# One hybrid decoder step on one core: order of the prompt and decode work inside the merged attention loop

## The reference, cut to what matters

```python
# prompt, causal, query blocks of 128
s = einsum('bqhcd,bkhcd->bhcqk', qi, k) * scale      # c: the two sub-heads
a = softmax(where(kpos <= qpos, s, -inf), axis=-1)
w = a[:, :, 0] - lam * a[:, :, 1]
o = einsum('bhqk,bkhv->bqhv', w, v)
# decode, per sequence: past pages and the new tokens under one softmax
s_past = einsum('bqhcd,bkhcd->bhcqk', q, k_past) * scale
s_new = where(tril, einsum('bqhcd,bkhcd->bhcqk', q, k) * scale, -inf)
a = softmax(concatenate([s_past, s_new], axis=-1), axis=-1)
w = a[:, :, 0] - lam * a[:, :, 1]
o = einsum(w[..., :P], v_past) + einsum(w[..., P:], v)
```

## Time and profile before

| | |
|---|---|
| median of 3 runs | 2041.23 us (2040.16 to 2042.34) |
| the profiled execution's own time | 2040.47 us |
| its span | 2038.8 us |
| PE, DVE, ACT busy over the span | 91%, 48%, 30% |
| attention loop in the span | about 519 to 946 us |

### The profile page before, as it was taken

The page is one execution under the profiler, slowest core; times in us unless marked ns, Lnnn a source line. Parts: engine busy times, 40 slices in busy tenths (PEclk is TensorE's granted clock), DMA queues, the critical chain, the costliest instruction groups (busy, mean ns, idle before and its releaser), DMA issues. The chain is left out here.

```text
span 2038.8 us, 35290 instructions
## 1 busy us (share of the span) xinstructions
PE 1863.9 (91%) x13412; PEld 1718.4 (84%) x13412; DVE 971.9 (48%) x1356; ACT 608.9 (30%) x1086; POOL 397.2 (19%) x393
## 2 busy tenths in 40 slices
PE   4999999575899999996999999999999999998898
PEld 4999999463566767664898999999999999998798
DVE  4223730486677777775325334344334333436443
ACT  4113321442465655563322211111111111113320
POOL 1112420232123333332112011101101110104110
PEclk9999999696899999998999999999999999999899
DMA  4332640204799999987111111111111111110221
GB/s 141 97 85 76 156 114 21 65 3 145 247 329 348 360 337 366 356 257 228 32 42 52 47 47 32 52 43 49 45 42 42 42 53 42 32 54 20 85 64 44
DMA packets 201583, 239.02 MB, mean 117 GB/s; under 512 B 15425, under 2 KB 142354, under 8 KB 201426
## 3 DMA queue, kind: packets, MB, share of 16 engines
q1 hardware_dynamic: 180946, 169.75, 27.0%
q0 software_dynamic: 20480, 67.13, 9.7%
HBM read 215.44 MB, written 16.91 MB: 114 GB/s over the span
## 5 line engine op out<-in xcount | busy, mean ns | idle before, releaser
L150 PE MATMUL psum<-h_hi,w_hi 128*128 128x364 f32 x1248 | 278.7, 332 | 2.8 <-issue 2.8
L150 PE MATMUL psum<-h_lo,w_hi 128*128 128x364 f32 x1248 | 276.3, 330 | 0.0
L150 PE MATMUL psum<-h_hi,w_lo 128*128 128x364 f32 x1248 | 275.2, 328 | 0.0
L2078 ACT ACTIVATE w_hi<-w_raw 128x1024 fp32r<-128x1024 f32 x66 | 68.8, 1059 | 586.3 <-PE psum L150 565.5
L150 PEld LDWEIGHTS psum<-h_hi,w_hi 128*128 128x128 f32 x1248 | 215.4, 189 | 4.9 <-issue 4.2
L150 PEld LDWEIGHTS psum<-h_lo,w_hi 128*128 128x128 f32 x1248 | 217.1, 189 | 0.0
L150 PEld LDWEIGHTS psum<-h_hi,w_lo 128*128 128x128 f32 x1248 | 216.7, 188 | 0.0
L2054 POOL TENSOR_TENSOR w_raw<-w_raw,gains 128x1024 f32<-128x1024 f32 x42 | 80.5, 1916 | 652.2 <-DMA w_raw<-in_w_ffn_gate 353.0
L1163 POOL DMA_DIRECT2D dec_v<-in_cache_v x256 | 137.5, 537 | 316.6 <-issue 316.6
L150 PE MATMUL psum<-x_hi,w_hi 128*128 128x364 f32 x792 | 188.5, 347 | 9.7 <-DVE x_lo L1911 5.8
L150 PE MATMUL psum<-x_hi,w_lo 128*128 128x364 f32 x792 | 176.5, 331 | 0.0
(11 more groups left out here) (262 smaller groups left out, 2793.4 us busy)
## 6 DMA issues: line engine op xcount, KB each, us to landing
dec_k<-in_cache_k SPq DMA_DIRECT2D x256, 256.0 KB, 5.1
dec_v<-in_cache_v POOLq DMA_DIRECT2D x256, 256.0 KB, 5.2
w_raw<-in_w_in SPq DMA_DIRECT2D x25, 512.0 KB, 3.9
w_raw<-in_w_ffn_gate SPq DMA_DIRECT2D x22, 512.0 KB, 3.9
w_raw<-in_w_ffn_up SPq DMA_DIRECT2D x22, 512.0 KB, 3.8
w_raw<-in_w_ffn_down SPq DMA_DIRECT2D x22, 512.0 KB, 3.6
feat_swap<-feat_n SPq DMA_DIRECT2D x32, 136.5 KB, 2.4
x_in<-in_x_prompt SPq DMA_DIRECT2D x4, 1024.0 KB, 8.2
```

Source lines behind the costliest of these rows:

```text
L150: ins = pe.matmul(out[:, c, 0:SPAN], w(k), x(k)[:, c * SPAN:c * SPAN + SPAN], start=n == 0 and w is whi and x is xhi, stop=n == len(ks) - ...
L2078: act.activation(m.whi[:, slot], m.raw[:, u], ACT.Copy).then_inc(s["w_hi"], 1)
```

## The change

`score_new(b)` moves from step 8b+8 to step 8b+6, two steps ahead of the batch's end, and its place in the ring's order moves with it. `take_new(b)` moves to step 8b+7, behind `copy_scores`, and keeps the mask and its own reduction; the maximum over the nine columns and `negm` become a function of their own, `batch_max(b)`, in step 8b+9 between `max_scores` and `copy_scores`. On PE, `prompt_scores(t)` moves from before `score(t - 1)` to the end of the step, behind `values(v)`. DVE's order of the other calls stays.

```diff
+NEW_AT = NG - 2
@@ class Ring
-            b, last = divmod(t - NG, NG)
+            b, last = divmod(t - NEW_AT, NG)
             if last == 0 and 0 <= b < DB:
                 use(("new_s", b), "dve")
@@ PE
-                prompt_scores(t)
                 if 1 <= t <= NKV:
                     score(t - 1)
-                if t and t % NG == 0 and t // NG <= DB:
-                    score_new(t // NG - 1)
+                if t % NG == NEW_AT and t // NG < DB:
+                    score_new(t // NG)
                 if 0 <= v < NKV:
                     values(v)
+                prompt_scores(t)
@@ DVE
-                dve.tensor_reduce(mx[:, g:g + 1], S_BANK, AX.X, ALU.max)
+                ins = dve.tensor_reduce(mx[:, g:g + 1], S_BANK, AX.X, ALU.max)
+                if g == NG - 1:
+                    ins.then_inc(d["mx"], 1)
@@ take_new
                 dve.tensor_reduce(mx[:, NG:NG + 1], dst, AX.X, ALU.max).then_inc(d["mx"], 1)
-                dve.wait_ge(d["mx"], b * 2 + 1)
+
+            def batch_max(b):
+                dve.wait_ge(d["mx"], b * 3 + 2)
                 dve.tensor_reduce(ssum[:, 1:2], mx, AX.X, ALU.max).then_inc(d["mx"], 1)
-                dve.wait_ge(d["mx"], b * 2 + 2)
+                dve.wait_ge(d["mx"], b * 3 + 3)
                 dve.tensor_scalar(negm[:, b % 2:b % 2 + 1], ssum[:, 1:2], -SC, None, ALU.mult).then_inc(d["negm"], 1)
@@ DVE's steps
                 if 0 < t - 1 <= NKV and (t - 1) % NG == 0:
-                    take_new((t - 1) // NG - 1)
+                    batch_max((t - 1) // NG - 1)
                 if 0 <= t - 2 < NKV:
                     copy_scores(t - 2)
+                if (t - 1) % NG == NEW_AT and (t - 1) // NG < DB:
+                    take_new((t - 1) // NG)
```

## The result

The changed kernel takes 2079.01 us (median of 4, 2076.15 to 2081.25) against 2040.70 us (4 runs): ratio 1.0189, interval 1.0175 to 1.0203, slower by 38.3 us. The forecast was 2062, slower by 21, with a range up to 2078: the direction was right, the size was not. The profiled execution took 2078.96 us, its span is 2077.3 us against 2038.8, so 38.5 us of the loss can be read in it.

The account below looks back on a forecast made before the run. PE was taken to bound the loop. +5.7 us in 16 steps made 17.1 for steps 16 to 63; with 2.4, 0.5 and 0.7 elsewhere, +20.7 on 2040.47 and 0.76 to the median gave 2062 us, range 2048 to 2078.

Parts of the forecast that it names:

- The swap: Prompt scores moved to the step's end: values wait for DVE, 4.5 us more in 16 steps.
- 2.67 + M: Microseconds into a step when DVE frees the values; M, the prompt maxima's time on DVE, is 0.99 to 1.80.
- the waits for exponentials: Prompt scores' waits for ACT's exponentials vanish, minus 3.1 us in 16 steps.
- the steps that I called covered: Steps where six to eight blocks of values or a long transpose hide DVE's chain, so values do not wait.
- The new keys ahead: Steps 8b+7: third key transpose idles 2.25 or 1.76 us for the new keys; losses 2.4 and 1.9, 4.3 in 16 steps.
- The batch's end: negm and turn_new_p come as before; the saved 0.91 us becomes longer waiting at turn_new_p, one stretch of 2.1 to 2.3.
- I take nothing here: Batch ends put at no change in the sum, with bounds minus 0.3 and plus 0.3 us for each of seven.
- The clock: Rival: 15 stalls of 1.8 to 2.3 us lower PE's clock, up to 22 us; chance of over 7 us 0.15.
- the waits removed would not be replaced: Rival: DVE has cover after all, so the removed waits are pure gain, 2024 to 2031 us; chance 0.08.
- no net change: Rival: values' waits half as large and the new-key stall under a microsecond, 2037 to 2045 us; chance 0.05.
- only the swap costing: Rival: the new-key stall is no more than the step's ordinary values' wait, 2053 us; chance 0.09.
- the sum by that rule: By the skill's rule that waits between bursts throttle PE, all 15 stalls lower the clock: 2084 us.

Follow-up runs that it names:

- e8: The changed kernel with DVE taking the new keys in the step they are made and the small merge product issued eight times; 2056.50 us.
- e3: The changed kernel with DVE taking the new keys in the step they are made, ahead of the prompt's maxima; 2053.55 us.
- e4: The changed kernel with the small merge product issued eight times instead of once, filling PE's stall at batch ends; 2070.12 us.
- e1: The kernel before with only the prompt's scores moved behind the value products; new keys stay at the batch's end; 2061.95 us.
- e2: The changed kernel with the prompt's scores back ahead of score(t - 1), so only the new keys are ahead; 2045.86 us.
- e5: The changed kernel with the prompt's scores in their old place and take_new in its own step behind the prompt's maxima; 2044.69 us.
- e6: The changed kernel with prompt scores in their old place, take_new in its own step behind the maxima, and the merge product issued seven times; 2037.68 us.

## Why the forecast was too small

**The swap: right in mechanism, undersized.** The chain on DVE and its 2.67 + M hold to 0.02 us in the step shown, and the waits for exponentials went. By the forecast's steps the swap nets 4.5 plus the ordinary waits of steps 8b+7 (1.0 and 0.6) minus 3.1, so 3.0 us in 16 steps; e8 measured 3.8. Most of what is missing lies in the steps that I called covered: of these each of the four even ones (18, 22, 26, 30) is about 0.15 us longer. Before, scores to values took 0.88 us; now it takes 1.01 (step 34: 748.66 to 749.67 us), and 1.11 in the heavy step 36 shown above, and the values' first weight load waits for DVE's copy in 39 places. I also named the wrong line for the wait: in heavy steps `score` waits for `copy_scores` first (0.7 to 0.8 us), and only the remainder is seen at `values`.

**The new keys ahead: right.** The stalls came out somewhat shorter (2.06 and 1.58 us instead of 2.25 and 1.76), the steps' loss as forecast. Forecast 2.4 minus 1.0 and 1.9 minus 0.6, so 1.4 and 1.3 us above the wait that the steps have anyway; e3 against the changed kernel gives 1.41 and 1.41. Eight of them are 11.3 us.

**The batch's end: right as to the chain, wrong as to its price.** `negm` and `turn_new_p` came where they had been (4.85 against 4.83 us). "I take nothing here" was the step that failed. The clock fell at all seven ends, about 11 us that the sum puts at nothing; two more falls in steps 7 and 39 make it 14, of the 18 us by which the profiled executions miss the sum (38.5 against 20.7). One stall of 2.1 to 2.3 us in place of two of 0.9 to 1.0 is not the same to PE as the same idle time.

**The clock: the term left out.** The prediction gave it as a rival, at 1.0 to 1.5 us a fall, with up to 2084 if it fell at all fifteen stalls, and 0.15 for more than 7 us. It fell nine times, at 1.4 to 1.8 us (in step 7, read the same way, 1.2). The reason to leave it out was that PE had been nearly idle ahead of the one fall in the trace; the falls behind ordinary, busy steps show that this is not needed.

**The account.** Loop: the swap with the new keys made and taken early +16.2 us (e8 less before), the new keys' stall 8 x 1.41 = +11.3, and what is left, 435.2 - 393.8 - 16.2 - 11.3 = +13.9, for nine falls of the clock, 1.5 each. The same arithmetic closes for e4, which was not used for it: 426.8 - 410.0 = 16.8, of which 11.3 is the stall and 5.5 the four falls left in it (steps 7, 9, 23 and 39), 1.4 each. Starting 0.8 us later and, from group 55's values to the end, 3.7 us less make the span's 38.5. Of the 3.7, 1.6 lie between the values of groups 55 and 57 (steps 64 to 66), where the stall before `turn_new_p` is 1.75 instead of 2.14 us, and the kernel before had half clock behind it and this one has not. The steps behind them give 0.3 back, and 2.4 lie behind the last value product, in code that is the same; all profiles together spread over 3.2 us there, so these are not put down to the change.

**Rivals.** That the waits removed would not be replaced, no net change, and only the swap costing, each fell with its profile. The page "TensorE: Matmul & The Clock Gate" of the Trainium skill, in "HAM oscillation — how this bites in real kernels", tells of waits for DMAs between bursts that throttle the PE again. The nine falls agree in kind, but the waits told of there are longer than those here. The prediction calls 2084, a fall at all fifteen stalls, the sum by that rule; it is not, though it was nearer than mine.

What stays open: why the same stall lets the clock fall in one batch and not in the next (in the changed kernel 2.06 us in step 23 did not, 2.07 us in step 39 did), and why e3 had two falls at batch ends where the changed kernel had seven. That stalls bring the falls is shown by filling them; which of them do is not forecast by their length alone.

## What to carry to other kernels

When work is moved on one engine, list what stands *behind* its consumer in the other engine's queue: here the prompt's scores were late by two products for DVE, and DVE held four further operations behind them. Moving the consumer along (the maxima behind the two passes over the scores), together with the new keys taken early and ACT's new order at a batch's end, turned the same idea from 1.9% slower into 0.5% faster. Taken early alone made it 0.8% slower (e3); the other two were not run apart. Two short stalls are not the same as one long one: 0.9 and 1.0 us left the clock alone at all batch ends before, 1.8 to 1.9 us in one piece halved it at five of six. But two pieces are no safeguard, as e1 shows. The price stands in PE's *busy* time, not in its waits. When PE's share is 94% and the DMAs' is 1.0, look for waits for pages next: here they took part of the gain.

## What the runs showed of the hardware

- Half clock behind single stalls of 1.8 to 1.9 us (five of six batch ends, in e2 and again in e5), of 2.1 to 2.3 us (six of six in the changed kernel, two of six in e3), and at three batch ends of e1, with two stalls of 1.3 to 1.6 and 1.0 us close together. The stall of 1.61 us in step 9 brought it in the changed kernel and in e4, and in none of the five others that have it. Stalls of 1.58 us left the clock at 1.00 four times in the changed kernel.
- A fall costs 1.4 to 1.8 us here, and 2.8 once (e1, step 25): the 512-column score product takes 1.94 us instead of 1.06, `turn_p` 1.06 instead of 0.60.
- Useless products in the gap keep the clock: six of six ends with eight merges stayed at 1.00 in e4 and again in e8, six of six with seven in e6, and the kernel with more work is faster, 2070.1 against 2079.0 us and 2037.7 against 2044.7.
